# A block of a small model: the expert layer PEER computed in two phases, with its down matrix copied in DRAM

## What is computed

```python
s1, i1 = top_k(q1 @ keys1, 16); s2, i2 = top_k(q2 @ keys2, 16)   # per token and head, 8 heads, 128 keys a side
top_s, idx = top_k(s1[:, None] + s2[None, :], 16)                # idx = i1 * 128 + i2, one of 16384 experts
gate = softmax(top_s)
hid  = einsum('td,thkd->thk', x, u_tab[idx])                     # 128 chosen experts per token
coef = gelu(hid) * gate
y    = einsum('thk,thkd->td', coef, v_tab[idx])                  # u_tab, v_tab: 16384 x 1024
h    = h + gt2 * y
```

## Time and profile before

| | |
|---|---|
| median of 3 runs | 2377.49 us (2374.24 to 2381.0) |
| the profiled execution | 2380.78 us, its span 2379.0 us |
| TensorE busy | 2235.2 us, 94% |
| VectorE busy | 1405.1 us, 59% |
| ScalarE busy | 904.0 us, 38% |
| GpSimd busy | 111.4 us, 5% |
| moved by DMA | 525.84 MB, mean 221 GB/s |
| mean granted clock of TensorE | 0.966 |

### The profile page before, as it was taken

One profiled execution on the slowest core, in us unless ns is written; L12 is line 12 of the kernel. 1 busy time (PEld: TensorE's weight loads), 2 busy tenths in 40 slices (PEclk: granted clock), 3 DMA queues, 4 the chain that ended last, 5 costly groups with the idle time before them and its releaser, 6 DMA issues. The chain is left out here.

```text
span 2379.0 us, 44386 instructions
## 1 busy us (share of the span) xinstructions
PE 2235.2 (94%) x17385; PEld 1717.6 (72%) x17385; DVE 1405.1 (59%) x2700; ACT 904.0 (38%) x1680; POOL 111.4 (5%) x143
## 2 busy tenths in 40 slices
PE   6999899999799999999999998999999979999996
PEld 3885799967367888888888886975566568666663
DVE  3694677754998777777777776665211176552123
ACT  4463243321187555555555554552101045321011
POOL 1000000000000000000000000000211010011110
PEclk8998899999799999999999998999999999999998
DMA  8235400037877655555555557513999973169997
GB/s 315 86 142 205 153 21 13 11 151 266 284 248 257 193 190 187 190 193 190 190 187 191 194 191 264 200 37 133 418 418 419 405 303 142 67 245 418 418 418 290
DMA packets 130227, 525.84 MB, mean 221 GB/s; under 512 B 19176, under 2 KB 21400, under 8 KB 100631
## 3 DMA queue, kind: packets, MB, share of 16 engines
q1 hardware_dynamic: 114206, 494.06, 55.9%
q0 software_dynamic: 15872, 29.65, 3.7%
HBM read 526.29 MB, written 26.31 MB: 232 GB/s over the span
## 5 line engine op out<-in xcount | busy, mean ns | idle before, releaser
L254 PE MATMUL PS<-over,over 128*128 128x512 f32 (+1 forms) x1056 | 386.8, 366 | 7.3 <-ACT ring L720 3.0
L256 PE MATMUL PS<-over,over 128*128 128x512 f32 (+1 forms) x1056 | 384.0, 364 | 0.0
L255 PE MATMUL PS<-over,over 128*128 128x512 f32 (+1 forms) x1056 | 383.3, 363 | 0.0
L2097 DVE TENSOR_TENSOR over<-ring,over 128x1024 fp32r<-128x1024 f32 x256 | 307.1, 1221 | 6.4 <-ACT over L2093 3.3
L3374 PE MATMUL PS<-ring 128*32 128x256 f32 (+2 forms) x2288 | 293.6, 384 | 9.2 <-DMA ring<-in_w_gate 9.2
L2093 ACT CAST over<-ring 128x1024 fp32r<-128x1024 f32 x256 | 267.7, 1047 | 65.6 <-PE PS L256 61.1
L3374 PEld LDWEIGHTS PS<-ring 128*32 128x32 f32 (+2 forms) x2288 | 211.8, 144 | 91.1 <-issue 30.9
L254 PEld LDWEIGHTS PS<-over,over 128*128 128x128 f32 x1056 | 201.6, 191 | 38.2 <-issue 6.4
L2158 PE MATMUL PS<-over,over 128*128 128x512 f32 x896 | 224.8, 390 | 2.5 <-POOLq L3513 2.5
L255 PEld LDWEIGHTS PS<-over,over 128*128 128x128 f32 x1056 | 201.0, 190 | 32.0 <-issue 0.5
L256 PEld LDWEIGHTS PS<-over,over 128*128 128x128 f32 x1056 | 200.6, 190 | 32.2
(11 more groups left out here) (538 smaller groups left out, 3119.2 us busy)
## 6 DMA issues: line engine op xcount, KB each, us to landing
ring<-in_mod_w SPq DMA_DIRECT2D x64, 1024.0 KB, 5.4
ring<-in_peer_u SPq DMA_DIRECT2D x128, 512.0 KB, 3.5
ring<-in_peer_v SPq DMA_DIRECT2D x128, 512.0 KB, 4.6
ring<-in_w_gate SPq DMA_DIRECT2D x64, 1024.0 KB, 17.4
ring<-in_w_up SPq DMA_DIRECT2D x64, 1024.0 KB, 20.4
ring<-in_w_down SPq DMA_DIRECT2D x64, 1024.0 KB, 21.1
ring<-in_w_in SPq DMA_DIRECT2D x12, 2048.0 KB, 9.2
ring<-in_dn_w SPq DMA_DIRECT2D x8, 2048.0 KB, 8.0
```

The costliest lines, as they stand in the source:

```text
L254: nc.tensor.matmul(out, lhs[0], rhs[0], start=start, stop=False)
L255: nc.tensor.matmul(out, lhs[0], rhs[1], start=False, stop=False)
L256: return nc.tensor.matmul(out, lhs[1], rhs[0], start=False, stop=stop)
L2097: nc.vector.tensor_tensor(PSPL[s % 4][0][:, 1, :], PRAW[s % 4], PSPL[s % 4][1][:, 0, :], ALU.subtract).then_inc(s_lo, 1)
```

## The change

- The 64 MB of `peer_v` are copied in DRAM to `peer_vh_home`, whose rows are 96 words longer (1120 words, 4480 bytes). GpSimd issues 20 of the 64 copies in `dn_proj` and 44 in `dn_delta`.
- Tokens 0 to 95 ("few") take their down rows by gather; tokens 96 to 255 stay on TensorE. `G` is built for these 160 tokens alone: 40 groups instead of 64. The 24 chunks of `mod_w` go through four buffers, in another place; their loads start once the last chunk of `peer_route` is used.
- Phase 1 of `peer_experts`: `hid(0)` to `hid(127)` for all tokens. Gelu of the 160 tokens goes on to `G`, multiplied in place in fp32. Gelu of the 96 tokens is written, every four j, to the last 96 words of the rows in `peer_vh_home`.
- Phase 2, TensorE: `y(m)` in plain fp32, straight from `peer_v` (loaded in pairs of 1 MB, six deep) and `G`: four strips of 32 tokens (96 to 127) by 256 columns, and two products of 512 columns for tokens 128 to 255.
- Phase 2, GpSimd and VectorE: for each of the 128 choices one gather of 96 rows, one row for each token, into seven buffers. VectorE picks the token's own activation from the 96 words behind the row with the identity and multiplies it by the gate (`weight_of`), then adds row times weight to `y_row` (`down_row`). At the end two products with the identity and four strips put both results into the banks that the next stage reads.

```diff
+SP_T = 96
+DN_T = T - SP_T
+W_STEP = 12
+VW = D + SP_T
+ROW_AT = ((20480, 4), (28672, 3))
...
+        NCOPY, NCOPY0 = 64, 20
+        vh_home = nc.dram_tensor("peer_vh_home", (NK * NK, VW), F32).ap()
+        v_rows, s_vcopy = io["peer_v"].rearrange("a b d -> (a b) d"), sem("p_vcopy")
+
+        def copy_down(e, lo, hi):
+            at = NK * NK // NCOPY
+            for n in range(lo, hi):
+                e.dma_start(vh_home[n * at:n * at + at, 0:D], v_rows[n * at:n * at + at, :]).then_inc(s_vcopy, 16)
...
             e.wait_ge(s_dn2in, 96)
+            copy_down(e, 0, NCOPY0)
...
             e.dma_start(ngb, io["dn_ng"].unsqueeze(0).broadcast_to([P, P])).then_inc(s_ng, 16)
+            copy_down(e, NCOPY0, NCOPY)
             e.wait_ge(s_ng, 16)
...
+            few = slice(0, SP_T)
+            c(V.scalar_tensor_tensor(row_hid[few], sel[few, 0, 0, :], float(NK), sel[few, 1, 0, :], ALU.mult, ALU.add))
+            c(V.tensor_copy(row_no[few], row_hid[few]))
+            c(V.tensor_copy(row_gate[few], sel[few, 2, 0, :]))
...
-        G = arena(0, NK, T)
+        G = arena(0, NK, DN_T)
...
+        WBUF = 4
+        w_buf = [chunk_view(arena(at, CHUNK)) for at in (20480, 22528, 24576, 28672)]
...
-            w_at.setdefault(3 + (m * 5) // 2, []).append(m)
+            w_at.setdefault(1 + (m * W_STEP) // 8, []).append(m)
...
+            pq_pe.wait(sp, ("l", NG0 * KC - 1))
...
-        PRAW = [ring[:, q * PW:(q + 1) * PW] for q in range(4)]
-        PSPL = [r32(4 * PW + q * 2 * PW, 2, PW) for q in range(4)]
...
+        NRAWU, NHB = 4, 4
+        u_raw = [ring[:, q * PW:(q + 1) * PW] for q in range(NRAWU)]
+        u_split = [r32(NRAWU * PW + q * 2 * PW, 2, PW) for q in range(NRAWU)]
...
+        NST = 4
+        h_stage = arena(26624, 2, NST, SP_T)
+        h_rows = vh_home[:, D:VW].rearrange("(i j) t -> i j t", i=NK)
+        NDEEP = 6
+        v_pair = [ring[:, 2 * PW * q:2 * PW * q + 2 * PW].rearrange("p (a d) -> p a d", a=2) for q in range(NDEEP)]
+        row_buf = [arena(at + q * VW, VW)[few] for at, n in ROW_AT for q in range(n)]
+        NROW = len(row_buf)
+        y_row, y_strip, kept = arena(25600, D)[few], arena(32128, 2 * P), arena(32384, SP_T)[few]
...
+            for j in range(NK):
+                if j >= NRAWU:
+                    sp.wait_ge(s_lo, j - NRAWU + 1)
+                sp.dma_start(u_raw[j % NRAWU], io["peer_u"][j]).then_inc(s_up[j % NRAWU], 16)
+            for p in range(NK // 2):
+                q = p % NDEEP
+                if p >= NDEEP:
+                    sp.wait_ge(s_y, 2 * (p - NDEEP) + 2)
+                elif q < 2:
+                    sp.wait_ge(s_lo, NK - 2 * (1 - q))
+                else:
+                    sp.wait_ge(s_hid, NK - NDEEP + 1 + q)
+                sp.dma_start(v_pair[q], io["peer_v"][:, 2 * p:2 * p + 2, :]).then_inc(s_down[q], 16)
+                if p == 40:
+                    sp.dma_start(peer_gb, io["final_g"].unsqueeze(0).broadcast_to([P, D])).then_inc(s_fin, 16)
+                    sp.dma_start(gain_mix, io["ng_mix0"].unsqueeze(0).broadcast_to([P, D])).then_inc(s_lin[0], 16)
+                    for q in range(2):
+                        sp.wait_ge(s_hst[q], HST0 + 16 * (NK // NST // 2))
+                    load_mod_now(sp, 0, 0)
...
+            for g in range(NK // NST):
+                e.wait_ge(s_few, NST * g + NST)
+                e.dma_start(h_rows[:, NST * g:NST * g + NST, :], h_stage[:, g % 2]).then_inc(s_hst[g % 2], 16)
+            for q in range(2):
+                e.wait_ge(s_hst[q], HST0 + 16 * (NK // NST // 2))
+            e.wait_ge(s_vcopy, 16 * NCOPY)
+
+            def down(r):
+                if r >= NROW:
+                    e.wait_ge(s_gone, r - NROW + 1)
+                e.indirect_dma_start(out=row_buf[r % NROW], out_offset=None, in_=vh_home,
+                                     in_offset=bass.IndirectOffsetOnAxis(ap=row_no[few, r:r + 1], axis=0),
+                                     bounds_check=NK * NK - 1, oob_is_err=False).then_inc(s_row[r % NROW], 16)
+            for r in range(NK):
+                down(r)
+                if r == NK // 2:
+                    e.wait_ge(s_hid, NK)
+                    e.dma_start(X.rearrange("p t d -> p (t d)"), x_home).then_inc(s_px, 16)
             e.wait_ge(s_px, 32)
...
+            e.wait_ge(s_gone, NK)
...
+            def half(j):
+                b = j % NHB
+                e.wait_ge(s_hid, j + 1)
+                if j >= NHB:
+                    e.wait_ge(s_coef, j - NHB + 1)
+                    e.wait_ge(s_few, j - NHB + 1)
+                nc.scalar.copy(act_h[:, b, :], PS[:, hid_bank[b], T:2 * T]).then_inc(s_half, 1)
+
+            def gelu(j):
+                b, g = j % NHB, j // NST
+                e.wait_ge(s_sum, j + 1)
+                nc.scalar.activation(act_h[:, b, SP_T:T], act_h[:, b, SP_T:T], ACT.Gelu).then_inc(s_gelu, 1)
+                if j % NST == 0 and g >= 2:
+                    e.wait_ge(s_hst[g % 2], HST0 + 16 * (g // 2))
+                nc.scalar.activation(h_stage[:, g % 2, j % NST, :], act_h[:, b, few], ACT.Gelu).then_inc(s_few, 1)
+            up_high(e, 1)
+            for j in range(NK):
+                if j + 2 < NK:
+                    up_high(e, j + 2)
+                if j >= 1:
+                    gelu(j - 1)
+                half(j)
+            gelu(NK - 1)
...
+            def sums(j):
+                b = j % NHB
+                e.wait_ge(s_half, j + 1)
+                V.tensor_tensor(act_h[:, b, :], act_h[:, b, :], PS[:, hid_bank[b], 0:T], ALU.add).then_inc(s_sum, 1)
+
+            def coefs(j):
+                e.wait_ge(s_gelu, j + 1)
+                V.tensor_tensor(G[:, j, :], act_h[:, j % NHB, SP_T:T], G[:, j, :], ALU.mult).then_inc(s_coef, 1)
+
+            def weight_of(r):
+                e.wait_ge(s_row[r % NROW], 16 * (r // NROW + 1))
+                if r:
+                    e.wait_ge(s_hot, r)
+                V.scalar_tensor_tensor(kept, row_buf[r % NROW][:, D:VW], row_gate[few, r:r + 1], ident[few, few], ALU.mult, ALU.mult,
+                                       accum_out=row_hid[few, r:r + 1]).then_inc(s_hot, 1)
+
+            def down_row(r):
+                buf, w = row_buf[r % NROW][:, 0:D], row_hid[few, r:r + 1]
+                e.wait_ge(s_hot, r + 1)
+                if r == 0:
+                    V.tensor_scalar(y_row, buf, w, None, ALU.mult).then_inc(s_gone, 1)
+                else:
+                    e.wait_ge(s_gone, r)
+                    V.scalar_tensor_tensor(y_row, buf, w, y_row, ALU.mult, ALU.add).then_inc(s_gone, 1)
+            up_low(e, 1)
+            for j in range(NK):
+                if j + 2 < NK:
+                    up_low(e, j + 2)
+                if j >= 1:
+                    coefs(j - 1)
+                sums(j)
+            coefs(NK - 1)
+            weight_of(0)
+            for r in range(NK):
+                if r + 1 < NK:
+                    weight_of(r + 1)
+                down_row(r)
...
+            def strips(m, v):
+                for j in range(4):
+                    ins = nc.tensor.matmul(PS[32 * j:32 * j + 32, 3, 0:STRIP], G[:, m, 0:32],
+                                           v[:, m % 2, STRIP * j:STRIP * j + STRIP], start=m == 0, stop=m == NK - 1,
+                                           tile_position=(0, 32 * j))
+                if m == NK - 1:
+                    ins.then_inc(s_end, 1)
+
+            def y(m):
+                p, q = m // 2, m // 2 % NDEEP
+                v = v_pair[q]
+                e.wait_ge(s_down[q], 16 * (p // NDEEP + 1))
                 e.wait_ge(s_coef, m + 1)
-                v, cf = PSPL[s % 4][0], coef[:, mm % 2]
-                for t in range(NT):
-                    for h in range(2):
-                        cols, tk = slice(h * CW, (h + 1) * CW), slice(t * P, (t + 1) * P)
-                        ins = exact3(PS[:, 4 + 2 * t + h, :], (cf[:, 0, tk], cf[:, 1, tk]), (v[:, 0, cols], v[:, 1, cols]),
-                                     start, stop)
-                ins.then_inc(s_use, 1)
+                if SP_T < P:
+                    strips(m, v)
+                for h in range(2):
+                    ins = nc.tensor.matmul(PS[:, 6 + h, :], G[:, m, P - SP_T:DN_T], v[:, m % 2, h * CW:(h + 1) * CW],
+                                           start=m == 0, stop=m == NK - 1)
+                ins.then_inc(s_y, 1)
             e.wait_ge(s_xlo, 1)
...
-            hid(0, 0, 0, 0)
-
-            def body(m, n, mm):
-                hid(m + 1, n, 2 * mm + 1, mm + 1)
-                y(m, n + 1, 2 * mm + 2, mm, start=mm == 0)
-            pairs(e, body)
-            y(NK - 1, NPART - 1, NPART - 1, NK - 1, stop=True)
-            e.wait_ge(s_use, NPART)
...
+            for j in range(NK):
+                hid(j)
+            for m in range(NK):
+                y(m)
+            e.wait_ge(s_gone, NK)
+            for h in range(2):
```

(20 more changed lines are left out.)

170 lines of the change are left out of this document (54 added, 116 removed).

## The result

The changed kernel takes 2483.48 us (median of 4 runs, 2469.09 to 2494.12) against 2377.94 before (4 runs, 2374.24 to 2381.0): ratio 1.044, 95% interval 1.038 to 1.050. It is slower; 2316 was forecast. The profiled execution took 2469.09 us, its span 2467.2.

The account below looks back on a forecast made before the run. TensorE's products were taken to bound peer_experts and VectorE peer_weights; after the change, transfers bind phase 2. Savings of 37 + 27 us less 2 for the copy, off 2377.5, gave 2316 us (range 2298 to 2335; 8 in 10: 2284 to 2372).

Parts of the forecast that it names:

- Phase 1, 356 us: peer_experts: the up products alone on TensorE, 128 x 2.77 us plus about 1.5 us for the low-clock start.
- The down step, 2.17 us: Phase 2, TensorE: two full-width products at 0.86 us and four strips at 0.45 us a step, 278 us for 128.
- At the 418 GB/s of the earlier trace that is 300 us: Phase 2, DMA: 125 MB of matrix, gathers and vectors at 418 GB/s; transfers, not TensorE, are the bound.
- Both signs: Phase 2, signs of being wrong: DMA rate well under 418 GB/s, or gather rows over 2.6 us apart.
- The tail at VectorE's pace: End of phase 2: the last 35 gathers go at VectorE's 1.7 to 2.1 us each, 60 to 73 us.
- Rival 2: Phase 2: gathers to partitions 0 to 95 fill one half of SBUF more; result 2366 us, chance 0.18.
- Rival 3: Phase 2: VectorE and GpSimd exclude each other both ways, 3.1 us a row, result 2404 us; chance 0.08.
- peer_weights, 27 us: peer_weights: ends at 727 instead of 754.9, set by the mod_w transfers; 27 us saved, bounds 15 to 34.
- The copy "cost at nothing": dn_proj and dn_delta: the DRAM copy of the down matrix costs nothing at low DMA share; 2 us in the sum.
- rival 4: dn_delta: a copy under 192 GB/s holds the norm_g1 load; at 130 GB/s 2430 us; chance 0.05.
- micro2's theory (b): Gathers: rows ending in each group of 8 partitions count; leaving out the last 32 is slow, near 300 GB/s.
- (a): Gathers: sixteen DMA engines take equal runs of rows; 96 of 128 run over 400 GB/s, 96-wide stay near 300.

Follow-up runs that it names:

- wide_pairs: wide_moved with the strips of both rows of a pair issued together, ahead of the four full-width products: 2372.22 us, ratio 0.997 to the kernel before.
- wide: The changed kernel with each 96-row gather asked for over all 128 partitions, the last 32 row numbers out of range: 2403.32 us, ratio 1.009.
- centred: The changed kernel with the 96 gathered rows sent to partitions 16 to 111 instead of 0 to 95: 2479.59 us, ratio 1.041.
- micro: The changed kernel with phase 2 replaced by twelve stretches of transfers alone, one execution: 315 GB/s with 96 rows of 4480 bytes beside the stream.
- before_copy: The kernel before plus only the 64 copies of the down matrix, into a buffer nobody reads: 2410.97 us, ratio 1.013.
- copy_moved: The changed kernel with 40 copies in dn_proj, 24 in phase 1 and none in dn_delta: 2446.98 us, ratio 1.029.
- copy_paced: The changed kernel with each copy in dn_delta issued only when the one before has landed: 2485.19 us, ratio 1.045.
- micro2: Changed kernel, phase 2 replaced by twelve other transfer stretches, 4608-byte rows, TensorE and VectorE idle, one execution: 417 GB/s with the last 32 of 128 out of range.
- wide_moved: wide with the copies placed as in copy_moved: 2370.02 us, ratio 0.997 to the kernel before.
- fourth: wide_pairs with every fourth token left to TensorE and out of range instead of the last 32, rows of 4608 bytes: 2333.64 us, ratio 0.982.
- rows_4608: The changed kernel with copied rows of 4608 bytes instead of 4480 and activations written in 512-byte pieces: 2481.99 us, ratio 1.043.

## Why the prediction was wrong, step by step

- **Phase 1, 356 us**: right. 359.3.
- **The down step, 2.17 us**: mis-sized, 2.48. The four full-width records are 1.72 as forecast; the missing 0.31 us is TensorE's change between strips and full width. wide_pairs, with half as many changes, gave back 0.16. As 128 x 0.31 = 40 us it would have turned 316 into about 330 (an estimate), since TensorE would have bound phase 2.
- **"At the 418 GB/s of the earlier trace rows that is 300 us"**: this step failed. The engines moved 303, and a choice came every 4.0 to 4.3 us instead of 2.4. Phase 2 took 1548.8 - 1123.7 = 425 us, 109 more than forecast. wide takes 80 of them back with the same bytes, so what the sum lacked was a rate for a transfer of 96 partitions. Both signs that the prediction named for being wrong came: a rate well under 418, and rows more than 2.6 us apart.
- **The tail at VectorE's pace**: right in kind, 1.6 us a row (1.7 to 2.1 forecast), but some 50 rows long instead of 35.
- **Rival 2 (one half of SBUF, 2366, 0.18)** named the 96 partitions but not the mechanism, and priced it too low: centred puts 48 rows on each side and stays slow, wide puts 64 and 32 and is 80 us faster.
- **Rival 3 (VectorE and GpSimd)**: wrong. VectorE's work takes the rate from 315 to 301 GB/s in micro; a gather beside it takes 1.28 us instead of 0.96, nearly always in the tail, where 1.28 + 0.30 is no longer than VectorE's 1.6. A row there takes 1.6 us and not 3.1, so the two engines do not exclude each other.
- **peer_weights, 27 us**: 21, within the bounds of 15 to 34; bound by the chunks of `mod_w` (DMA share 1.01) as the working had it.
- **The copy "cost at nothing"**: this failed too, by 34 us in `dn_delta` against 2. Its rate was as forecast, above 192 GB/s (48.19 MB of it in 238 us, and it was through by 416), and rival 4 is wrong: it never reached `norm_g1`. I counted the engines' room and the queue behind it. Nobody waits for the copies; TensorE stops for 2 to 3 us at a time with nothing to wait for. before_copy shows that the copies alone do this (33 us), copy_moved that it goes with them, copy_paced that it shrinks when only one is on its way. What is late is TensorE's own instructions. Between two gaps stand 125 or 126 of its product records, or two or three times as many; here 16 + 32 + 64 + 14:

```profile
299.46 3.94 PE L1175 MATMUL PS<-ring 64*64 64x64 f32 x126 [1.69 <-issue]
306.18 0.68 PE L1175 MATMUL PS<-ring 64*64 64x64 f32 x16 [2.77 <-issue]
306.69 1.10 PE L1214 MATMUL PS<-ring 64*64 64x64 f32 x32
307.62 2.03 PE L1175 MATMUL PS<-ring 64*64 64x64 f32 x64
309.49 0.63 PE L1223 MATMUL PS<-ring 64*64 64x64 f32 x14
312.62 0.73 PE L1223 MATMUL PS<-ring 64*64 64x64 f32 x17 [2.51 <-issue]
```

The trace's DMA packets have the other half. The instruction queue q8 brings 137 packets of 16384 bytes in the execution, one for 251 of TensorE's 34410 records of products and weight loads. Every gap of over 0.6 us from 250 to 420 ends 1.2 to 1.5 us behind the end of such a packet (304.87 and 311.43 before the two ends above), and so it is in before_copy, in copy_paced, and at the two short gaps of the kernel before. A packet takes about 1 us with the copies and without; it comes late, and what holds it back is not shown. `dn_delta` takes 42 such packets in 293 us, `dn_proj` 8 in 196, phase 1 17 in 359. That the small instructions make the difference and not the load shows in `dn_proj`, where 20 copies fill the engines as well and TensorE has no gap (columns as in the earlier trace rows):

```profile
90.00:130.00 40.00, 40.00 (x178) 33.14 (x177) 29.75 (x37) 20.70 (x44) 0.00 (x0) 1.00 1.02 364
```

The sum of the forecast for this execution was 2380.8 - 62 = 2318.8. Phase 1 and 2 add 112; `dn_delta` adds 29, which is 34 less the 3 gained before it and the 2 that the forecast had for the copy; `peer_weights` adds 6, and 3 come behind: 2469, where 2469.1 was measured.

Open: why rows that all lie in the first three quarters of a 128-wide transfer ran at 417 GB/s in micro2 and at 367 in wide_moved, where the stream is paced by TensorE. That twelve of sixteen engines carry them was the reasoning that led to fourth, and its number came out (2335 expected); but the DMA share in wide_moved is 0.97, which does not show a quarter of the engines idler than the rest. That the last 32 left out were slower there than every fourth is what micro2's theory (b) would have, though it wanted 300. By (a)'s reckoning micro2's stretch would need 297/16 + 120/12 = 28.6 GB/s of each of the twelve (13.35 MB of stream and 5.41 MB of rows in 45 us), more than 418/16 = 26; with six loads under way the other four may have run ahead for so short a stretch, which no run tests. Nor was fourth's spread tried apart from its longer rows, though these alone did nothing in rows_4608.

## What to carry to other kernels

A rate read from full-width loads is not the rate of a transfer of another width: here gathers of 96 partitions and the full-width loads beside them came to some 300 GB/s together instead of 418, at a DMA share of 1.0, so compare GB/s and not the share. If a gather needs fewer rows, ask for all 128 and put the rest out of range, spread evenly. Work that nobody waits for can still cost where an engine runs through thousands of small instructions, since these are loaded by DMA too; put it beside long ones.

## What the runs showed of the hardware that I had not expected

- The stream falls from 421 GB/s to 250 on 96 partitions, and to 208 on partitions 0 to 63; beside the stream 96 rows give 305 to 316, 128 rows 416 to 418, 64 rows into 32 to 95 415.
- Row numbers out of range cost no transfer time: 96 rows of 128 at 415 GB/s.
- 46 MB of DRAM-to-DRAM copies, about 310 GB/s, cost TensorE 26 us of gaps in 154 us of `dn_delta`. They cost none in phase 1, where copy_moved ran them at about 95 GB/s, and none in `dn_proj` at a full DMA load.
- TensorE's gaps without a visible wait end 1.2 to 1.5 us after a 16 KB packet of its instruction queue.
- TensorE changes between 32-column strips and full-width fp32 products at a cost of about 0.31 us for there and back.
